# Two transformer blocks in one Trainium2 kernel: the silus of the first attention computed from the hyperbolic tangent, and its splits, gatings and table load at other steps

## The chip, the cores and the metric

The kernel runs on one core of a Trainium2 chip. The metric is the device time of one execution in microseconds (us), taken as the median of several runs. Five engines work side by side, each through its own queue in order: TensorE (PE in the profile, with its weight loads as PEld), VectorE (DVE), ScalarE (ACT), GpSimd (POOL) and SyncE (SP), which here only issues DMAs. They wait for each other through semaphores that count upwards.

## The reference, cut to what matters

A first block (a norm, one input projection, eight heads of a top-k attention "a" and eight heads of a dilated attention "b", a gating and an output projection) is followed by a second block and a final norm. What the change touches is the gating of the first block. `za` and `zb` are two slices of the input projection, and in the reference the attention output is multiplied by their silu before the output projection:

```python
def first_block(...):
    ...
    gated = concat(out_a, out_b) * silu(concat(za, zb))     # the gating, in short
    x = x + gated @ w_out
```

silu(z) is z * sigmoid(z), which equals z * 0.5 * (1 + tanh(z / 2)). Everything is float32; the kernel gets float32 accuracy on TensorE by writing each operand as a high part (fp32r) and a low part (the difference), and by three products: high with high, high with low, low with high.

## The kernel before, in words

Every engine's program is written out by hand in one function, `build`. The first attention is a loop over 64 steps (`steps1`), one step for one head and one tile of 128 queries: 8 groups of 8 steps, the first four groups for branch b and the last four for branch a. In a group the key width grows from 128 to 512 columns (two steps of each). All engines walk the steps in pairs (t = 0, 2, 4 ...):

- PE, step pair t: the scores of t and t+1 (`pair1`), which need that VectorE has taken the scores before them (`l_done`); then "fill" work, which is the projection of one of the eight tiles `zb 0..3`, `za 0..3` (`FILL1`), cut into single k chunks of three matmuls; then the transposes of the scaled probabilities of steps t-4 and t-3 (`turn1`, L1096); every fourth step the products with the values (`value1`, L1111). The transposes go alternately to two PSUM banks, so that the transpose of step u waits until VectorE has taken out the one of step u-2 (`t_free`, set by `turned_low`, L2222).
- ACT, step pair t: `turned_high(t-4)`, `turned_high(t-3)` (L1761, the high part of the transposed probabilities), `exps(t)`, `exps(t+1)` (L1578), sometimes `low_rows_of` (L1768), then what the tables put at t and t+1: `silu`, `high` (the high part of a weight unit, L1613), `wo_high` (the high part of a piece of `w_out`, L1747), and last `mixed_high` (L1730).
- DVE, step pair t: `score1(t)` (L2269), the reciprocal of the sums of t-2 and t-1 (L2277), `score1(t+1)`, `collect1` (L2230), `mix` (the gating, L2238), `gate_rows` (L2247 and L2248), `mixed_low` (L2254), `low` (the low part of a weight unit, L2090), `wo_low` (L2260), and then `turned_low(t-4)`, `turned_low(t-3)`.
- POOL, step u: the scaling of the probabilities by the reciprocal (L2752), which must be done before `turn1(u)`; in branch a also `combine(u+4)` (bias plus mask, L2739), which must be done before `score1(u+4)`; and at two steps `output_low` (L2746).
- SP: the loads. Weight unit number F0+n belongs to tile n of `FILL1`. Units F0+2 and later may be loaded only when PE has finished the tile two before it (`raw_free`), since they take its place in the ring.

The steps at which things happen are dictionaries from step to item. PE has filled the eight tiles at steps 8, 18, 26, 34, 41, 47, 53 and 59. `silu(tile)` runs in place on `zT` after `gate_rows`. `Silu` needs another activation table than `Exp`, and the silus were called in four pairs, at steps 20, 36, 49 and 63. The units' `high` parts were made at steps 10, 20, 28, 36, 43 and 49 (units F0+2 to F0+7), their `low` parts at step pairs 12, 22, 30, 38, 44 and 50, and that of F0+1 at 0. PE needs the units F0+1 to F0+7 at steps 10, 18, 27, 35, 42, 48 and 54.

Of the kernel before, what the change touches and what calls it, by code (L numbers as in the profile page):

```python
# [29 lines left out]
F32 = mybir.dt.float32  # L30
# [11 lines left out]
NH = 8  # L42
# [128 lines left out]
def build(nc, w, out):  # L171
# [29 lines left out]
    HIGH1 = {filled[tile] + 2: unit_of[tile] + 2 for tile in FILL1 if unit_of[tile] + 2 < U2}  # L201
    LOW1 = {1: F0 + 1, **{step // 2 * 2 + 2: u for step, u in HIGH1.items()}}
    GATE_AT = {tile: max(filled[tile], HALF + 8) if tile[0] == "za" else filled[tile] for tile in FILL1}

    SILU_AT = {min(filled[FILL1[2 * n + 1]] + 2, NS - 1) if n < 3 else NS - 1: n for n in range(4)}
    MIX_AT = {22: 0, 24: 1, 38: 2, 40: 3, 50: 4, 56: 5, 64: 6}
# [42 lines left out]
    with ExitStack() as ctx:  # L249
# [204 lines left out]

        def wo_raw(n, k, count=1):
            if n == 0:
                return v1["vb"][:, k:k + count, :] if k < 4 else qk1[:, 0, k - 4:k - 4 + count, K_LO, :]
            return late_raw[k // 2][:, k % 2:k % 2 + count, :] if k < 4 else qk1[:, 0, k - 4:k - 4 + count, OUTS, :]
# [96 lines left out]
        ki_lo_done = sem("ki_lo_done")  # L555
        z_done = sem("z_done")
# [938 lines left out]
        def _(act):  # L1495
# [213 lines left out]
            for g, done in zip(HEADED, (None, "kb", "qb", None, "ka", "qa")):  # L1709
                for k in range(3):  # L1710
                    if g != "va":
                        high(unit_of[(g, k)] + HI_UNITS)
                    if g == "kb":
                        for h in range(IDX_HEADS):
                            index_relu(k + 1, h)
                    if done is not None and k > 0:
                        head_high(done, 2 * k - 2)
                        head_high(done, 2 * k - 1)
                if g == "va":
                    high(F0)  # L1720
                for i in LAST_ORDER[g]:
                    take((g, i))
                high(F0 + 1 if g == "va" else unit_of[(g, 3)] + HI_UNITS)
                if g[0] != "v":
                    head_root(g)

# [22 lines left out]
            def silu(tile):  # L1749
                act.wait_ge(a_free, AT[tile] + 1)  # L1750
                z = zT[:, (0 if tile[0] == "za" else 4) + tile[1], :]
                run(z, z, ACT.Silu).then_inc(z_done, 1)
# [17 lines left out]
            for t in range(0, NS + 4, 2):  # L1770
# [10 lines left out]
                for u in (t, t + 1):  # L1781
                    if u in SILU_AT:
                        for n in range(2):
                            silu(FILL1[2 * SILU_AT[u] + n])
                    if u in HIGH1:
                        high(HIGH1[u])
                    if u in WO_HIGH:
                        wo_high(WO_HIGH[u])
# [255 lines left out]
        def _(dve):  # L2044
# [41 lines left out]
            def low(u):  # L2086

                dve.wait_ge(u_hi_done, u + 1)
                cols = unit_cols(u)
                v.tensor_tensor(u_lo[raw_place(u)][:, 0:cols], raw_unit(u),  # L2090
                                u_hi[hi_place(u)][:, 0:cols].bitcast(F32), ALU.subtract).then_inc(u_lo_done, 1)
# [142 lines left out]
            def mix(o, cols=slice(0, S)):  # L2234
# [3 lines left out]
                v.tensor_tensor(zT[:, k, cols], zT[:, k, cols], qk1[:, o // 4, o % 4, OUTS, cols], ALU.mult).then_inc(gated_done, 1)  # L2238

            def gate_rows(tile):  # L2240

                n = AT[tile]
                z = zT[:, (0 if tile[0] == "za" else 4) + tile[1], :]
# [28 lines left out]
            for t in range(0, NS + 4, 2):  # L2272
# [24 lines left out]
                for u in (t, t + 1):  # L2297
                    if u in LOW1:
                        low(LOW1[u])
# [387 lines left out]
        def _(pool):  # L2687
# [60 lines left out]

            for u in range(NS):
                if u % 2 == 0:  # L2750
                    pool.wait_ge(rden_done, u // 2 + 1)
                g.tensor_scalar(logits1[u % 8], logits1[u % 8], den[:, u:u + 1], unit_factor, ALU.mult, ALU.mult).then_inc(scaled, 1)  # L2752
                if u in (9, 11, 13, 15):
# [161 lines left out]
```

## Time and profile before

| what | value |
|---|---|
| median of 3 runs | 1031.36 us (1031.04 to 1031.43) |
| the profiled execution, its own time | 1029.16 us |
| its span in the trace | 1027.3 us |
| PE busy | 1005.7 us, 98% of the span |
| DVE, ACT, POOL busy | 680.4, 563.2, 422.8 us |
| mean granted TensorE clock | 0.999 |

How to read it: the span is the time between the first and the last instruction of the trace, and the profiled execution's own time is 1.9 us more. A busy engine counts only its work, not its waits. The first attention lies from about 170 to 300 us of the span. A row of a timeline gives start, duration, engine, source line, operation, tiles written and read, the shape, and in brackets how long the engine had been idle before it and who ended that. In the names, `x` is where the probabilities lie, `consts<-bank` is `low_rows_of`, and `arena<-arena` is a gating or a silu.

### The profile page before, as it was taken

The page shows a single profiled execution, that of the slowest core. Times are in us where ns is not written, and L with a number is a line of the kernel's source. Part 1 is how long each engine was busy: PE and PEld are TensorE (multiplying, and loading weights), DVE is VectorE, ACT ScalarE, POOL GpSimd, SP SyncE. Part 2 cuts the span into 40 slices and gives each one's busy share as a digit, 9 for nine tenths or more (in the row PEclk, how much of TensorE's full clock was granted, in tenths as well). Part 3 has the DMA queues.
Part 4 walks back from the last instruction along what each step waited for, and adds up shares of the span by engine and source line. Part 5 has one row for each costly group of instructions (what it writes and reads, how often), then busy time and mean ns, then how long its engine had stood idle before and what let it go on. Part 6 is the DMA issues. An engine that isn't in the chain of part 4 may idle for free. (4 is left out here: it accounts for less than half of the span.)

```text
span 1027.3 us, 14257 instructions
## 1 busy us (share of the span) xinstructions
PE 1005.7 (98%) x5150; PEld 826.2 (80%) x5150; DVE 680.4 (66%) x1207; ACT 563.2 (55%) x1032; POOL 422.8 (41%) x407
## 2 busy tenths in 40 slices
PE   9999999999989999999999999999999999999997
PEld 7788877777778898878887788888888888888885
DVE  5578997788974446824567879454322325999997
ACT  8455445778873355544567884234433446554564
POOL 0024011557840002900264430007779965874562
PEclk9999999999999999999999999999999999999999
DMA  9433321336140384233200362239999941443552
GB/s 336 104 98 109 88 67 36 83 83 191 56 175 1 103 267 143 60 82 83 63 2 1 121 229 62 82 111 323 347 352 349 356 168 62 153 143 135 205 185 82
DMA packets 100166, 146.25 MB, mean 142 GB/s; under 512 B 6480, under 2 KB 60496, under 8 KB 100096
## 3 DMA queue, kind: packets, MB, share of 16 engines
q1 hardware_dynamic: 86800, 130.75, 38.9%
q10 hardware_dynamic: 12768, 12.88, 4.0%
q0 software_dynamic: 528, 1.70, 0.9%
q8 instruction: 41, 0.67, 0.3%
q14 instruction: 29, 0.24, 0.1%
HBM read 123.69 MB, written 21.63 MB: 141 GB/s over the span
## 5 line engine op out<-in xcount | busy, mean ns | idle before, releaser
L2578 DVE TENSOR_TENSOR w_lo<-wring,w_hi 128x1024 fp32r<-128x1024 f32 x32 | 51.4, 1607 | 107.5 <-ACT w_hi L1944 107.5
L2090 DVE TENSOR_TENSOR u_lo<-wring,u_hi 128x1024 fp32r<-128x1024 f32 (+1 forms) x64 | 82.5, 1296 | 53.6 <-ACT u_hi L1613 52.9
L935 PE MATMUL bank<-u_hi,h_hi 128*128 128x512 f32 (+1 forms) x288 | 110.9, 385 | 0.1
L935 PE MATMUL bank<-u_hi,h_lo 128*128 128x512 f32 (+1 forms) x288 | 109.3, 379 | 0.0
L935 PE MATMUL bank<-u_lo,h_hi 128*128 128x512 f32 (+1 forms) x288 | 109.0, 378 | 0.0
L1613 ACT ACTIVATE u_hi<-wring 128x1024 fp32r<-128x1024 f32 (+1 forms) x64 | 66.2, 1034 | 69.4 <-PE bank L935 54.7
L935 PE MATMUL bank<-h_hi,w_hi 128*128 128x512 f32 (+2 forms) x272 | 103.2, 379 | 0.0
L935 PE MATMUL bank<-h_hi,w_lo 128*128 128x512 f32 (+2 forms) x272 | 103.1, 379 | 0.0
L935 PE MATMUL bank<-h_lo,w_hi 128*128 128x512 f32 (+2 forms) x272 | 103.1, 379 | 0.0
L935 PE MATMUL bank<-h_hi,u_hi 128*128 128x512 f32 x224 | 93.8, 419 | 0.4 <-ACT arena L1555 0.2
L1441 PE MATMUL bank<-s_hi,f_hi 128*128 128x512 f32 x224 | 87.4, 390 | 0.7 <-DVE f_lo L2612 0.7
L935 PE MATMUL bank<-h_lo,u_hi 128*128 128x512 f32 x224 | 87.7, 391 | 0.0
L935 PE MATMUL bank<-h_hi,u_lo 128*128 128x512 f32 x224 | 87.7, 391 | 0.0
L1442 PE MATMUL bank<-s_hi,f_lo 128*128 128x512 f32 x224 | 87.2, 389 | 0.0
L1443 PE MATMUL bank<-s_lo,f_hi 128*128 128x512 f32 x224 | 87.2, 389 | 0.0
L1944 ACT ACTIVATE w_hi<-wring 128x1024 fp32r<-128x1024 f32 x32 | 33.9, 1060 | 91.9 <-PE bank L935 91.9
L2804 POOL TENSOR_SCALAR arena<-arena,stats 128x128 f32<-128x128 f32 (+3 forms) x64 | 40.5, 642 | 95.0 <-DVE stats L2534 94.8
L2752 POOL TENSOR_SCALAR x<-x,stats 128x128 f32<-128x128 f32 (+3 forms) x64 | 49.4, 777 | 53.9 <-DVE stats L2277 53.9
L2604 DVE TENSOR_TENSOR s_lo<-wring,s_hi 128x2048 fp32r<-128x2048 f32 (+1 forms) x32 | 67.8, 2119 | 5.6 <-ACT s_hi L1974 5.6
L935 PEld LDWEIGHTS bank<-u_hi,h_hi 128*128 128x128 f32 x288 | 54.1, 188 | 11.5 <-issue 1.2
L935 PEld LDWEIGHTS bank<-u_lo,h_hi 128*128 128x128 f32 x288 | 54.1, 188 | 10.2
L1974 ACT ACTIVATE s_hi<-wring 128x2048 fp32r<-128x2048 f32 (+1 forms) x32 | 54.3, 1696 | 14.0 <-PE bank L1443 13.8
(382 smaller groups left out, 2600.2 us busy)
## 6 DMA issues: line engine op xcount, KB each, us to landing
wring<-in_w_in SPq DMA_DIRECT2D x60, 512.0 KB, 3.9
wring<-in_w_ff ACTq DMA_DIRECT2D x12, 1024.0 KB, 8.7
wring<-sums_kept SPq DMA_DIRECT2D x16, 768.0 KB, 4.2
wring<-in_w_ff SPq DMA_DIRECT2D x22, 512.0 KB, 6.2
wring<-in_w_ff SPq DMA_DIRECT2D x32, 256.0 KB, 3.3
sums_kept<-wring SPq DMA_DIRECT2D x22, 256.0 KB, 5.2
wring<-in_w_out SPq DMA_DIRECT2D x2, 2048.0 KB, 13.2
wring<-in_w_ff SPq DMA_DIRECT2D x4, 1024.0 KB, 6.9
```

Of the source, the lines that this page charges most:

```text
L935: last = mm(b, lhs, rhs, start=(start and n == 0), stop=(stop and n == 2))
L1441: mm(b, f[0][:, token], w[0][:, high], start=start, stop=False)
L1442: mm(b, f[1][:, token], w[0][:, high], start=False, stop=False)
L1443: return mm(b, f[0][:, token], w[1][:, lows], start=False, stop=stop)
L1613: run(u_hi[hi_place(u)][:, 0:unit_cols(u)], raw_unit(u), ACT.Copy).then_inc(u_hi_done, 1)
L1944: run(dst, src, ACT.Copy).then_inc(w_hi_done, 1)
L1974: run(s_hi[m % 4][:, 0:PAIR - at], pair_raw(m)[:, at:PAIR], ACT.Copy).then_inc(s_hi_done, 1)
L2090: v.tensor_tensor(u_lo[raw_place(u)][:, 0:cols], raw_unit(u), u_hi[hi_place(u)][:, 0:cols].bitcast(F32), ALU.subtract).then_inc(u_lo_done, 1)
L2578: v.tensor_tensor(cut(w_lo[ring3(m)]), src, cut(w_hi[ring3(m)]).bitcast(F32), ALU.subtract).then_inc(w_lo_done, 1)
L2604: v.tensor_tensor(s_lo[pair_place(m)][:, at:PAIR], pair_raw(m)[:, at:PAIR], s_hi[m % 4][:, 0:PAIR - at].bitcast(F32), ALU.subtract)
L2752: g.tensor_scalar(logits1[u % 8], logits1[u % 8], den[:, u:u + 1], unit_factor, ALU.mult, ALU.mult).then_inc(scaled, 1)
L2804: g.tensor_scalar(place, place, den2[:, u:u + 1], gates[:, i, at:at + 1], ALU.mult, ALU.mult).then_inc(scaled, 1)
```

## The change

- `silu` becomes `half_tanh`: ScalarE computes tanh(z/2) with `Tanh` and scale 0.5 into a place of its own (`tanh_place`, where a chunk of K's high part has been), waits for that on its own semaphore, adds 1 with `Identity` and a bias of one, and signals `tanh_done`. Before the first it waits until VectorE has taken every score of that chunk of heads (`l_done`), since PE reads that chunk until then. Tiles zb0 to zb3 and za0 to za3 come at steps 10, 20, 28, 36, 42, 48, 54 and 60, one at a time.
- GpSimd multiplies z with 1 + tanh (`gated`), behind the scaling of steps 12, 21, 29, 37, 45, 53, 61 and 62, and signals `z_done`.
- `mix` multiplies z with the attention output and with 0.5, by `scalar_tensor_tensor` in place of `tensor_tensor`. The gatings 0 to 3 move from steps 22, 24, 38, 40 to 18, 32, 34, 40, and with them `mixed_high` (two steps later) and `mixed_low` (four steps later). The others stay.
- The units' `high` parts come at steps 9, 19, 27, 35, 41 and 47, and so one step pair earlier than before.
- The units' `low` parts can be made in halves: F0+1 at 4 and 6 (before: 0), F0+2 at 10 (12), F0+3 at 20 and 22 (22), F0+4 at 28 and 30 (30), F0+5 at 38 (38), F0+6 at 42 and 46 (44), F0+7 at 50 (50).
- The table for `Exp` is asked for after the projection of `qa` instead of by the first `Exp`.

```diff
-    HIGH1 = {filled[tile] + 2: unit_of[tile] + 2 for tile in FILL1 if unit_of[tile] + 2 < U2}
-    LOW1 = {1: F0 + 1, **{step // 2 * 2 + 2: u for step, u in HIGH1.items()}}
+    HIGH1 = {filled[tile] // 2 * 2 + 1: unit_of[tile] + 2 for tile in FILL1 if unit_of[tile] + 2 < U2}
+    LOW1 = {4: (F0 + 1, 0), 6: (F0 + 1, 1), 10: (F0 + 2, None), 20: (F0 + 3, 0), 22: (F0 + 3, 1), 28: (F0 + 4, 0), 30: (F0 + 4, 1),
+            38: (F0 + 5, None), 42: (F0 + 6, 0), 46: (F0 + 6, 1), 50: (F0 + 7, None)}
...
-    SILU_AT = {min(filled[FILL1[2 * n + 1]] + 2, NS - 1) if n < 3 else NS - 1: n for n in range(4)}
-    MIX_AT = {22: 0, 24: 1, 38: 2, 40: 3, 50: 4, 56: 5, 64: 6}
+    TANH_AT = {10: 0, 20: 1, 28: 2, 36: 3, 42: 4, 48: 5, 54: 6, 60: 7}
+    GATED_AT = {12: 0, 21: 1, 29: 2, 37: 3, 45: 4, 53: 5, 61: 6, 62: 7}
+    MIX_AT = {18: 0, 32: 1, 34: 2, 40: 3, 50: 4, 56: 5, 64: 6}
...
+        def tanh_place(tile):
+            return qk1[:, 0 if tile[0] == "zb" else 1, tile[1], MIX_LO, :]
...
+                if g == "qa":
+                    nc.scalar.preload_act_table(ACT.Exp)
...
-            def silu(tile):
+            def half_tanh(tile):
                 act.wait_ge(a_free, AT[tile] + 1)
-                z = zT[:, (0 if tile[0] == "za" else 4) + tile[1], :]
-                run(z, z, ACT.Silu).then_inc(z_done, 1)
+                act.wait_ge(l_done, (0 if tile[0] == "zb" else HALF) + NH * (tile[1] + 1))
+                run(tanh_place(tile), gate_place(tile), ACT.Tanh, scale=0.5).then_inc(half_tanh_done, 1)
+                act.wait_ge(half_tanh_done, FILL1.index(tile) + 1)
+                run(tanh_place(tile), tanh_place(tile), ACT.Identity, bias=unit_factor).then_inc(tanh_done, 1)
...
-                    if u in SILU_AT:
-                        for n in range(2):
-                            silu(FILL1[2 * SILU_AT[u] + n])
+                    if u in TANH_AT:
+                        half_tanh(FILL1[TANH_AT[u]])
...
-            def low(u):
+            def low(u, part=None):
 
                 dve.wait_ge(u_hi_done, u + 1)
-                cols = unit_cols(u)
-                v.tensor_tensor(u_lo[raw_place(u)][:, 0:cols], raw_unit(u),
-                                u_hi[hi_place(u)][:, 0:cols].bitcast(F32), ALU.subtract).then_inc(u_lo_done, 1)
+                size = unit_cols(u) // (1 if part is None else 2)
+                cols = slice((part or 0) * size, (part or 0) * size + size)
+                done = v.tensor_tensor(u_lo[raw_place(u)][:, cols], raw_unit(u)[:, cols],
+                                       u_hi[hi_place(u)][:, cols].bitcast(F32), ALU.subtract)
+                if part != 0:
+                    done.then_inc(u_lo_done, 1)
...
-                v.tensor_tensor(zT[:, k, cols], zT[:, k, cols], qk1[:, o // 4, o % 4, OUTS, cols], ALU.mult).then_inc(gated_done, 1)
+                v.scalar_tensor_tensor(zT[:, k, cols], zT[:, k, cols], 0.5, qk1[:, o // 4, o % 4, OUTS, cols], ALU.mult, ALU.mult)\
+                    .then_inc(gated_done, 1)
...
+            def gated(tile):
+                pool.wait_ge(tanh_done, FILL1.index(tile) + 1)
+                z = gate_place(tile)
+                g.tensor_tensor(z, z, tanh_place(tile), ALU.mult).then_inc(z_done, 1)
...
+                if u in GATED_AT:
+                    gated(FILL1[GATED_AT[u]])
```

## Rows read from the trace of the kernel before

**Rows 1.** The page, busy time of the engines.
```profile
PE 1005.7 (98%) x5150; PEld 826.2 (80%) x5150; DVE 680.4 (66%) x1207; ACT 563.2 (55%) x1032; POOL 422.8 (41%) x407
```
**Rows 2.** Busy time by stretch: start, length, PE, PEld, DVE, ACT, POOL, clock, DMA.
```profile
245.00:262.00 17.00, 15.59 (x103) 12.45 (x102) 15.61 (x46) 14.36 (x33) 15.06 (x15) 1.00 0.55 151
...
sum 130.00, PE 120.00 PEld 95.09 DVE 106.30 ACT 103.25 POOL 83.30; mean PE 20.00 PEld 15.85 DVE 17.72 ACT 17.21 POOL 13.88
```
**Rows 3.** Waits of PE from 165 to 300: total, times, longest.
```profile
PE bank L1096 <- DVE pt_lo L2222: 4.5, 6, 1.3
PE bank L1086 <- DVE stats L2269: 3.9, 6, 1.4
```
**Rows 4.** Timeline of PE, instructions in front of which it stood idle.
```profile
175.24 0.79 PE L1086 MATMUL bank<-qk_half 64*128 64x384 f32 x6 [1.18 <-DVE stats L2269]
...
193.96 0.95 PE L1086 MATMUL bank<-qk_half 64*128 64x128 f32 x12 [0.71 <-DVE stats L2269]
...
209.83 0.85 PE L1096 MATMUL bank<-consts,x 128*128 128x128 f32 x6 [0.89 <-DVE pt_lo L2222]
...
214.18 1.09 PE L1096 MATMUL bank<-consts,x 128*128 128x128 f32 x8 [0.52 <-DVE pt_lo L2222]
...
254.81 0.96 PE L1086 MATMUL bank<-qk_half 64*128 64x128 f32 x12 [1.39 <-DVE stats L2269]
...
265.89 0.30 PE L1096 MATMUL bank<-consts,x 128*128 128x128 f32 x1 [1.05 <-DVE pt_lo L2222]
...
292.37 1.09 PE L1096 MATMUL bank<-consts,x 128*128 128x128 f32 x8 [1.35 <-DVE pt_lo L2222]
```
**Rows 5.** Groups by line and shape, 190 to 320: busy us, mean ns, idle before.
```profile
L2739 POOL TENSOR_TENSOR junk<-arena,x 128x512 f32<-128x512 f32 x8 | 10.3, 1285 | 0.0
...
L2090 DVE TENSOR_TENSOR u_lo<-wring,u_hi 128x1024 fp32r<-128x1024 f32 x9 | 12.5, 1391 | 3.5 <-ACT u_hi L1613 3.2
...
L1752 ACT ACT_TABLE_LOAD x4 | 5.1, 1283 | 0.1
...
L1752 ACT ACTIVATE arena<-arena 128x512 f32<-128x512 f32 x8 | 4.6, 624 | 0.0
```
**Rows 6.** DMA issue of unit F0+2, and its time from issue to landing.
```profile
L739 SPq DMA_DIRECT2D wring<-in_w_in x1: 368/368/368, 182.1 to 182.1; - x1
...
DMA to landing us min/median/max: 4.6/4.6/4.6
```
**Rows 7.** The same of unit F0+6.
```profile
L739 SPq DMA_DIRECT2D wring<-in_w_in x1: 424/424/424, 240.7 to 240.7; - x1
...
DMA to landing us min/median/max: 7.4/7.4/7.4
```
**Rows 8.** ACT at steps 9 to 10 and 40 to 43.
```profile
183.62 0.40 ACT L1578 ACTIVATE x<-x,stats 128x128 f32<-128x128 f32 x1
...
186.23 1.09 ACT L1761 ACTIVATE pt_hi<-bank 128x512 fp32r<-128x512 f32 x2 [2.13 <-PE bank L1096]
...
242.93 0.39 ACT L1578 ACTIVATE x<-x,stats 128x128 f32<-128x128 f32 x1
...
248.20 1.06 ACT L1613 ACTIVATE u_hi<-wring 128x1024 fp32r<-128x1024 f32 x1
```
**Rows 9.** PE, the transposes of steps 8 and 9, and of 40 and 41.
```profile
188.77 0.38 PE L1096 MATMUL bank<-consts,x 128*128 128x128 f32 x2
...
248.09 0.38 PE L1096 MATMUL bank<-consts,x 128*128 128x128 f32 x2
```
**Rows 10.** POOL: two scalings, the second behind a gap.
```profile
250.74 2.04 POOL L2752 TENSOR_SCALAR x<-x,stats 128x256 f32<-128x256 f32 x1
...
256.47 0.77 POOL L2752 TENSOR_SCALAR x<-x,stats 128x512 f32<-128x512 f32 x1 [1.16 <-DVE stats L2277]
```
**Rows 11.** DVE, score of step 63.
```profile
285.77 0.69 DVE L2269 CUSTOM_DVE_ANT_0 x<-bank,junk 128x512 f32<-128x512 f32 x1
```
**Rows 12.** ACT, the last exponential before the score of step 63.
```profile
283.81 0.61 ACT L1578 ACTIVATE x<-x,stats 128x384 f32<-128x384 f32 x1
```

More of the change, by code:

```diff
@@ L453, in build, with gate_place @@
         mix_place = lambda k: (0, k - 4) if k >= 4 else (1, k)
+        def gate_place(tile):
+            return zT[:, (0 if tile[0] == "za" else 4) + tile[1], :]
+        def tanh_place(tile):
+            return qk1[:, 0 if tile[0] == "zb" else 1, tile[1], MIX_LO, :]
         def wo_raw(n, k, count=1):
@@ L555, in build @@
         ki_lo_done = sem("ki_lo_done")
+        half_tanh_done = sem("half_tanh_done")
+        tanh_done = sem("tanh_done")
         z_done = sem("z_done")
@@ L2237, in mix @@
                 dve.wait_ge(z_done, FILL1.index(("zb" if k >= 4 else "za", k % 4)) + 1)
-                v.tensor_tensor(zT[:, k, cols], zT[:, k, cols], qk1[:, o // 4, o % 4, OUTS, cols], ALU.mult).then_inc(gated_done, 1)
+                v.scalar_tensor_tensor(zT[:, k, cols], zT[:, k, cols], 0.5, qk1[:, o // 4, o % 4, OUTS, cols], ALU.mult, ALU.mult)\
+                    .then_inc(gated_done, 1)
             def gate_rows(tile):
                 n = AT[tile]
-                z = zT[:, (0 if tile[0] == "za" else 4) + tile[1], :]
+                z = gate_place(tile)
                 if tile == ("za", 0):
@@ L2298, in _ @@
                     if u in LOW1:
-                        low(LOW1[u])
+                        low(*LOW1[u])
                     if WO_HIGH.get(u - 2, 5) < 5:
@@ L2747, in output_low @@
                     .then_inc(wo_lo_done, 1)
+            def gated(tile):
+                pool.wait_ge(tanh_done, FILL1.index(tile) + 1)
+                z = gate_place(tile)
+                g.tensor_tensor(z, z, tanh_place(tile), ALU.mult).then_inc(z_done, 1)
             for u in range(NS):
```

## The prediction

> **What bounds the kernel now.** I read the page first. PE is busy for 98% of the span [rows 1], so no change to ACT, DVE or POOL can be worth more than the idle time of PE in the stage it touches. The busy time by stretches gives that bound: in the 130 us of the first attention PE works 120 us, at full clock, so that 10 us are open; DVE and ACT work 106 and 103 us, and POOL 83 [rows 2]. From 245 to 262 all four are over 84% busy [rows 2]. There is hardly slack, and what is late on one engine soon reaches PE. The waits of PE tell by whom it is held: 4.5 us in six waits by `turned_low`, which must free the bank for the next transpose, and 3.9 us in six waits by `score1` [rows 3]. The timeline then says where. The reader is to see seven places with 1.18, 0.71, 0.89, 0.52, 1.39, 1.05 and 1.35 us [rows 4]; they make 7.1 of the 8.4 us. Only some belong to silus. The one at 175 stands behind the first `Exp`'s table load; 209.8 and 214.2 follow the silus of step 20, 265.9 those of step 49, 292.4 those of step 63. The one at 194 follows a unit's low part on DVE, and the one at 254.8 a late `combine` on POOL.
>
> **The change part by part.** All times below are on the clock of the old trace, and a gain or a loss is how much earlier or later PE gets through the same work.
>
> *Table load and the first low part.* A table load takes 1.28 us [rows 5]. The first `Exp` no longer waits for one, and DVE's low part of F0+1 (1.39 us [rows 5]) no longer stands in front of the scores of step 2. Asked for in the projection, the load lies where ACT waits for PE anyway; without that cover it would cost its 1.28 us. The wait of 1.18 us [rows 4] goes: -1.2 us. The two halves of 0.7 us at 4 and 6 lie in gaps of DVE.
>
> *Silu to tanh on ACT.* Four pairs cost 4.6 us of silu and 5.1 us of table loads [rows 5], and three more loads of 1.28 us back to `Exp` (3.8): 13.5 us. Sixteen activations of about 0.62 us [rows 5], and some 0.1 us for a wait on the own result, make 10.7 us. ACT gains 3 us in sum and loses its four knots of 2.6 to 5 us. At step 20 this frees PE: of 0.89 and 0.52 I take -1.4 us (bounds 0 and -1.9: nothing, if the low half and `mixed_low`, which stand before `turned_low` at 22, hold it as long; or also the short waits beside it).
>
> I weigh a rule here. The table load's rows show 1283 ns and the next activation starts at its end. The Trainium skill (ScalarE: Activation LUTs, What ACT_TABLE_LOAD costs) gives 1283 ns as well, but adds a drain and says 2.66 us for each switch. By the rows seven loads are 9.0 us of ACT, by the page they would be 18.6; I go by the rows, which show no drain.
>
> *The high parts one step pair earlier.* This is where I expect the loss, for `high` waits for a DMA that starts only when PE has finished a tile, and everything behind it on ACT's queue waits too. Unit F0+2 is issued at 182.1 and lands 4.6 us later, at 186.7 [rows 6]. Before, ACT came to it at step 10, at 188.8. Now it comes at step 9, after the exponentials that end at 184.0 [rows 8]: ACT stands for 2.7 us and then needs 1.05. `turned_high(6)` starts at 187.8 instead of 186.2 [rows 8]. DVE also stands, for its low part at pair 10 waits for the high part (187.8) and takes 1.39 us [rows 5]; two `turned_low` of about 0.65 us end at 189.9 and 190.5. PE wants the transposes of 8 and 9 at 188.8 [rows 9] and gets the second at 190.5: +1.7. The tanh of zb0 adds 1.3 us behind it on ACT, in time for the next transposes. The wait at 194 (0.71 [rows 4]) came from the low part at pair 12 and is partly used up: net +1.0 us (bounds +0.3 and +1.5).
>
> F0+3, F0+4 and F0+5 have the queue to themselves, as F0+2 has, and land about when ACT arrives at steps 19, 27 and 35, where it has had `low_rows_of` in front: nothing, for the `high` then takes the place of waits of ACT for PE (up to +0.5 each if not).
>
> Unit F0+6 is the heavy one. It is issued at 240.7 and, behind 2 MB of `w_out` in the same queue, lands 7.4 us later, at 248.1 [rows 7]. Before, ACT started it at 248.2, at step 43, having hardly waited [rows 8]. At step 41 ACT comes at 243.3 [rows 8], or at 242.0 with its earlier steps. It stands for 5 to 6 us. Behind it wait `turned_high(38)` and (39), the exponentials of 42 and 43, the tanh of za0 and `mixed_high(3)`; DVE stands too, in the first half of the low part at pair 42. So: high part until 249.2; `turned_high(38)` 249.8; DVE's half low part 249.9, `turned_low(38)` 250.6, (39) 251.2. PE wants the transposes of 40 and 41 at 248.1 [rows 9], and before that would have been 0.4 earlier: it gets the second at 251.2, over 3 us late. Value products, scores and fills up to the scores of 48 need 5 us as before, so PE is there at 256.2, and DVE's score of 47 is out at 256.6. At step 48 the old wait of 1.39 us [rows 4] for POOL shrinks, since PE is late itself: 256.6 against 254.8, net +1.8 us (bounds 0, if PE has other work to do, and +3.5).
>
> F0+7 at step 47 lands before ACT reaches it, but stands before `wo_high(1)` and `turned_high(44)`; DVE's `wo_low(1)` stands behind that, and at pair 50 DVE still has gating, low part (1.39 us [rows 5]) and `wo_low` in front of `turned_low(46)`, about 3 us. So the gain from the silus of step 49 (1.05 [rows 4] and a second wait of 0.30) doesn't come out whole: +0.8 us (bounds -1.35 and +1.5).
>
> *The last tanh.* The tanh of za3 stands at step 60, but waits for the score of step 63, since it writes over K. That score ends at 286.5 [rows 11]; ACT has ended its exponentials of 60 and 61 at 284.4 [rows 12]. It stands for 2 us, then needs 1.3, and `wo_high`, `turned_high(58)`, (59) and the exponentials of 62 and 63 come 2.3 us late. By step 64 it is level with the old order, as two silus and their load (2.5 us [rows 5]) are gone there. But the exponentials are late for POOL, which now also has products in front of the scalings of 62 and 63 (1.29 us each [rows 5]), and `low_rows_of` ends only at 291.0; behind it on DVE stand `collect1`, gating 6 and `turned_low(60)`, 2.2 us. That is out at 293.2, and the transposes of 62 and 63 start at 293.2 instead of 292.4 [rows 4]: +0.9 us (bounds -1.0 and +2.5).
>
> *The products on GpSimd.* Eight of 1.285 us [rows 5], 10.3 us. Most stand where POOL waits for the next reciprocal (as the 1.16 us before 256.5 [rows 10]). The trace shows what they can do besides: a scaling of 256 columns took 2.04 us while DVE subtracted between SBUF tiles, one of 512 columns 0.77 [rows 10]. Each product may hold DVE, or be held, for up to 1.3 us. I take +0.4 us in all (bounds 0 and +5, half of the eight on the path). The gating by `scalar_tensor_tensor` has the same two SBUF inputs and columns as before; the trace has no such row with both in SBUF, and I take nothing (bounds: 0.1 us less or more for each of eight).
>
> The Trainium skill (SBUF — State Buffer, the physical ports) says that a VectorE instruction with two SBUF inputs and a GpSimd one that reads SBUF exclude each other for a whole instruction; by that rule, the trace agrees, with 2.04 for a scaling that the wider one did in 0.77. It speaks against the eight products: all on the path would be 10 us.
>
> *Sum.* -1.2 +1.0 -1.4 +1.8 +0.8 +0.9 +0.4 = +2.3 us. The profiled execution took 1029.16 us, which gives 1031.5; the median of the runs lies 2.2 above it, so 1033.7.
>
> **The rivals.** (1) *PE never feels the landings.* It ends on the other side. PE has the scores and the fills of a pair in hand, and the transposes wait for ACT with some slack. For it: ACT saves 3 us and its knots, and at 186 it had been idle for 2.1 us [rows 8]. Against it: banks are only two, and ACT's wait at step 41 is over 4.8 us. It decides if `turned_low(38)` ends by 248, which needs the landing 3 us earlier. Then: -1.2 +1.0 -1.4 -1.35 (265.9) -1.35 (292.4) = -4.3: 1027.1. (2) *The port.* Half of the products on the path, and scalings held by low parts: +5 more than the knots give, 1038. Speaks for it: 245 to 262 is nearly full on both [rows 2]. Against: their places are mostly gaps. (3) *Tanh doesn't share Exp's table.* The trace shows no tanh. Then there are 16 loads instead of 7 and a knot at each tile; even one us for each on PE gives +8, and 16 us of ACT at the most: 1042. (4) *Even.* Gains and losses cancel within a microsecond: 1031.4.
>
> The Trainium skill (ScalarE: Activation LUTs, Table sets: the hidden batching unit) puts tanh in the set of exp, so rival 3 is unlikely by it; no run here shows it yet.
>
> **How the numbers follow.** The forecast gets 0.50 with its own range 1031 to 1037, rival 1 0.25, rival 2 0.13, rival 3 0.04, rival 4 0.08. 0.2% is 2.1 us, about what a measurement of this kernel can tell. The forecast lies just outside of it: 0.28 slower, 0.20 within, 0.02 faster. Faster 0.27; same 0.20 + 0.08 = 0.28; slower 0.28 + 0.13 + 0.04 = 0.45. The range is 1026.8 to 1038.5: rival 1 with a little, and rival 2.
>
> **What would show it.** One table load before 170 and none between 175 and 300; no wait at 175; ACT idle for 2 to 3 us and for 5 to 6 us in front of `u_hi` L1613 (shifted lines) for units F0+2 and F0+6, released by the DMA; PE waiting about 3 us at the transposes of 40 and 41; ACT idle for about 2 us before the last tanh. It would be wrong if the unit lands early, if PE has work in between, or if the products stretch DVE's low parts and gatings by far more than 0.1 us each.

## The result, and the profile after

The changed kernel takes 1037.83 us (median of four runs, 1035.96 to 1040.39), the one before 1031.20 (1031.03 to 1031.43) beside it: a ratio of 1.0058, 95% interval 1.0042 to 1.0074. It is slower. Forecast were 1033.7, a range of 1026.8 to 1038.5, and slower as the likeliest of the three outcomes. The direction holds, the size is 4.1 us short: the time lies above the forecast's own range (1031 to 1037) and close to the 1038 of rival 2. The profiled execution took 1035.96 us, its span is 1034.1.

The busy time of the engines on the page after, beside [rows 1]:

```profile
PE 1008.9 (98%) x5150; PEld 828.8 (80%) x5150; DVE 681.0 (66%) x1211; ACT 558.8 (54%) x1033; POOL 436.9 (42%) x415
```

ACT has 4 us less to do and POOL 14 more, and that alone tells nothing. The busy time by stretch, beside [rows 2], does:

```profile
245.00:262.00 17.00, 12.59 (x84) 9.77 (x83) 12.01 (x31) 12.44 (x27) 11.63 (x14) 1.00 0.46 132
...
283.00:300.00 17.00, 13.36 (x77) 10.63 (x76) 12.14 (x30) 12.06 (x31) 15.29 (x16) 0.92 0.00 1
sum 130.00, PE 117.11 PEld 92.50 DVE 106.14 ACT 95.67 POOL 92.73; mean PE 19.52 PEld 15.42 DVE 17.69 ACT 15.95 POOL 15.45
```

From 245 to 262 PE works 12.6 of 17 us; before it worked 15.6 [rows 2]. All engines are less busy there, which is what a stretch looks like in which everything stands for one transfer. The last column but two of 283 to 300 is new: the granted clock of TensorE is 0.92, not 1.00.

PE's waits from 165 to 300, beside [rows 3]:

```profile
PE bank L1106 <- DVE pt_lo L2238: 9.6, 9, 2.5
PE bank L945 <- DVE u_lo L2104: 1.4, 1, 1.4
PE bank L945 <- POOL qk_half L2763: 1.0, 1, 1.0
PE bank L1096 <- DVE stats L2286: 0.6, 3, 0.2
```

The waits for scores fell from 3.9 us to 0.6; those for `turned_low` (L2238 now) rose from 4.5 to 9.6, and a wait for a unit's low part in `three` (L945, a fill) is new. (The transposes of `turn1` are L1106 now, the scores of `pair1` L1096, `high` L1623, `low` L2104.)

PE's timeline, where it stood idle, beside [rows 4]:

```profile
189.62 0.30 PE L1106 MATMUL bank<-consts,x 128*128 128x128 f32 x1 [0.90 <-DVE pt_lo L2238]
...
239.96 0.41 PE L1106 MATMUL bank<-consts,x 128*128 128x128 f32 x2 [1.08 <-DVE pt_lo L2238]
...
250.15 0.30 PE L1106 MATMUL bank<-consts,x 128*128 128x128 f32 x1 [2.48 <-DVE pt_lo L2238]
...
258.51 0.50 PE L945 MATMUL bank<-h_hi,u_hi 128*128 128x512 f32 x1 [1.39 <-DVE u_lo L2104]
```

The wait of 1.18 us at 175 is gone, and so are those at 209.8 and 214.2. The ones at 189.6 and 250.2 are the two that were forecast, behind F0+2 and F0+6: ACT stood for the load of the unit, and what PE needed stood behind it. Those at 240.0 and 258.5 were not.

To count gains and losses I take PE's matmuls by their number, 5150 in both traces, and subtract the start of each before from its start after. At some numbers (first line: the time in the old trace), in us:

```
old time       173.7  175.2  188.9  194.0  217.9  239.9  244.7  248.2  250.8  254.8  255.7  265.9  292.4  300.6  end
after           1.07  -0.18   1.35   0.79  -1.10   0.05  -0.43   2.55   2.67   1.36   2.82   3.57   4.87   5.67  6.81
```

I call these numbers offsets; only how an offset changes from one place to the next tells of a loss or a gain. 1.07 of it is there before the first changed instruction acts, and 1.14 comes after the first attention; between them lie 4.6 us.

ACT's timeline at the two landings and before the last tanh (a number in brackets is the idle time in front, and what ended it), beside [rows 8, 12]:

```profile
186.56 1.06 ACT L1623 ACTIVATE u_hi<-wring 128x1024 fp32r<-128x1024 f32 x1 [2.65 <-DMA wring<-in_w_in]
...
247.62 1.06 ACT L1623 ACTIVATE u_hi<-wring 128x1024 fp32r<-128x1024 f32 x1 [5.48 <-DMA wring<-in_w_in]
...
289.92 0.63 ACT L1764 ACTIVATE arena<-arena 128x512 f32<-128x512 f32 x1 [2.07 <-DVE stats L2286]
```

All engines in front of the two waits of PE that were not forecast (timeline, 236 to 240 and 256 to 259):

```profile
236.67 1.73 POOL L2769 TENSOR_TENSOR arena<-arena 128x512 f32<-128x512 f32 x1
...
237.17 2.31 DVE L2104 TENSOR_TENSOR u_lo<-wring,u_hi 128x1024 fp32r<-128x1024 f32 x1
...
239.40 0.74 DVE L2238 TENSOR_TENSOR pt_lo<-bank,pt_hi 128x256 fp32r<-128x256 f32 x2
...
256.64 1.27 POOL L2769 TENSOR_TENSOR arena<-arena 128x512 f32<-128x512 f32 x1
256.70 1.77 DVE L2104 TENSOR_TENSOR u_lo<-wring,u_hi 128x512 fp32r<-128x512 f32 x1
```

A low part of 1024 columns took 1.39 us in the mean of before [rows 5]; here it takes 2.31, and a half of 512 columns takes 1.77. Each time a product on POOL (L2769) has begun just before, and DVE is through about when a low part of normal length would be that had waited for the product's end (238.40 and 257.91). Behind it stand the `turned_low` or the fill for which PE waits: 1.15 and 1.46 us in the table.

The kernel before has such a pair already, where GpSimd makes a low part of the values (L2722), and so the price could have been read there. Its trace has (timeline, two places)

```profile
189.86 1.28 POOL L2722 TENSOR_TENSOR va_both<-arena,va_both 128x512 fp32r<-128x512 f32 x1
189.96 2.27 DVE L2090 TENSOR_TENSOR u_lo<-wring,u_hi 128x1024 fp32r<-128x1024 f32 x1
...
251.23 1.21 DVE L2090 TENSOR_TENSOR u_lo<-wring,u_hi 128x1024 fp32r<-128x1024 f32 x1
```

2.27 us where GpSimd's instruction had begun 0.1 us before, and 1.21 where it was GpSimd's scaling that took longer (2.04 us [rows 10]).

The Trainium skill (SBUF — State Buffer, SBUF: two separate sides) has the rule that was weighed in the prediction, and adds that whichever of the two engines starts first keeps the ports for its whole instruction. These rows agree.

Groups by line and shape, 190 to 320:

```profile
L2769 POOL TENSOR_TENSOR arena<-arena 128x512 f32<-128x512 f32 x8 | 10.7, 1335 | 0.0
...
L1766 ACT ACTIVATE arena<-arena,stats 128x512 f32<-128x512 f32 x8 | 5.8, 724 | 0.3
...
L1764 ACT ACTIVATE arena<-arena 128x512 f32<-128x512 f32 x8 | 5.0, 622 | 2.1 <-DVE stats L2286 2.1
...
L2254 DVE SCALAR_TENSOR_TENSOR arena<-arena 128x512 f32<-128x512 f32 x7 | 7.9, 1124 | 0.1
```

The products and the sixteen activations cost what was taken for them, nearly: 10.7 us on POOL against 10.3, and 10.8 on ACT against 10.7. What the products do to others is another matter: a gating on DVE takes 1124 ns in the mean, where the kernel before had 864.

Last, busy time by stretch around the place where the granted clock of TensorE fell:

```profile
293.50:297.17 3.67, 1.67 (x12) 1.18 (x10) 2.87 (x6) 2.33 (x6) 3.10 (x3) 1.00 0.00 0
297.17:300.58 3.41, 3.34 (x13) 3.09 (x14) 2.99 (x7) 1.96 (x5) 2.67 (x3) 0.50 0.04 11
300.58:304.00 3.42, 3.42 (x24) 3.12 (x24) 1.96 (x4) 2.62 (x6) 1.32 (x1) 1.00 0.93 367
```

PE had been busy for 1.67 of 3.67 us. Then the clock was 0.50 for 3.41 us, which is 1.2 GHz instead of 2.4: 13 matmuls where the next 3.42 us hold 24. The trace of the kernel before has no such stretch until 1025, when the work ends.

The four runs of the changed kernel, each with the mean granted clock of the run, get longer as it falls:

```
us       1035.96  1037.30  1038.36  1040.39
clock    0.997    0.995    0.993    0.992
```

The runs of before that stood beside the experiments (75 in three sets) have 0.999 in the median. They show the same: the 43 at 0.999 took 1030.5 us in the median, the 11 at 0.997 took 1033.0. So the kernel before has executions in which the clock falls too.

### The profile page after: what moved, and what is told of

Read it like the earlier page. It is cut to its first block and busy times, and to the rows that moved or that the text cites. A ratio compares the mean times of both kernels' runs of the same rounds, so it can differ in the third digit from the quotient of the medians.

```text
span 1034.1 us, 14278 instructions
## 1 busy us (share of the span) xinstructions
PE 1008.9 (98%) x5150; PEld 828.8 (80%) x5150; DVE 681.0 (66%) x1211; ACT 558.8 (54%) x1033; POOL 436.9 (42%) x415
## 5 line engine op out<-in xcount | busy, mean ns | idle before, releaser
L2104 DVE TENSOR_TENSOR u_lo<-wring,u_hi 128x1024 fp32r<-128x1024 f32 (+2 forms) x68 | 84.2, 1246 | 59.9 <-ACT u_hi L1623 59.1
L945 PE MATMUL bank<-u_hi,h_hi 128*128 128x512 f32 (+1 forms) x288 | 110.9, 385 | 0.1
L945 PE MATMUL bank<-u_hi,h_lo 128*128 128x512 f32 (+1 forms) x288 | 109.2, 379 | 0.0
L945 PE MATMUL bank<-u_lo,h_hi 128*128 128x512 f32 (+1 forms) x288 | 109.0, 378 | 0.0
L1623 ACT ACTIVATE u_hi<-wring 128x1024 fp32r<-128x1024 f32 (+1 forms) x64 | 66.2, 1035 | 79.0 <-PE bank L945 55.6
L945 PE MATMUL bank<-h_hi,w_hi 128*128 128x512 f32 (+2 forms) x272 | 103.2, 379 | 0.0
L945 PE MATMUL bank<-h_hi,w_lo 128*128 128x512 f32 (+2 forms) x272 | 103.1, 379 | 0.0
L945 PE MATMUL bank<-h_lo,w_hi 128*128 128x512 f32 (+2 forms) x272 | 103.1, 379 | 0.0
L945 PE MATMUL bank<-h_hi,u_hi 128*128 128x512 f32 x224 | 93.8, 419 | 1.8 <-DVE u_lo L2104 1.4
L945 PE MATMUL bank<-h_hi,u_lo 128*128 128x512 f32 x224 | 87.7, 391 | 0.0
L945 PE MATMUL bank<-h_lo,u_hi 128*128 128x512 f32 x224 | 87.6, 391 | 0.0
L945 PEld LDWEIGHTS bank<-u_hi,h_hi 128*128 128x128 f32 x288 | 54.1, 188 | 11.5 <-issue 1.2
L945 PEld LDWEIGHTS bank<-u_lo,h_hi 128*128 128x128 f32 x288 | 54.1, 188 | 10.2
L945 PEld LDWEIGHTS bank<-u_hi,h_lo 128*128 128x128 f32 x288 | 54.1, 188 | 9.4
```

Source lines behind the costliest of these rows:

```text
L945: last = mm(b, lhs, rhs, start=(start and n == 0), stop=(stop and n == 2))
L1623: run(u_hi[hi_place(u)][:, 0:unit_cols(u)], raw_unit(u), ACT.Copy).then_inc(u_hi_done, 1)
L2104: done = v.tensor_tensor(u_lo[raw_place(u)][:, cols], raw_unit(u)[:, cols], u_hi[hi_place(u)][:, cols].bitcast(F32), ALU.subtract)
```

## The experiments

Twelve kernels, five rounds each against the kernel before; four kernels at a time ran on one chip, each four on another. The ratio is the measure, for before's median is 1030.8 to 1031.1 us from one set to the next. "Offset" is how much later than in the old trace PE starts the same matmul, as in the table above.

**e1. The heavy landing alone.** The changed kernel with F0+6 at its old steps:

```
+    HIGH1[43] = HIGH1.pop(41)
-            ... 42: (F0 + 6, 0), 46: (F0 + 6, 1), 50: (F0 + 7, None)}
+            ... 44: (F0 + 6, None), 50: (F0 + 7, None)}
```

> The changed kernel with the high part of unit F0+6 back at step 43 and its low part whole at pair 44. Theory L (landing: high parts that come before their DMA hold ACT): ACT no longer stands in front of that high part, PE gets the transposes of 40 and 41 about 3.0 us earlier, 1.2 us of it comes back as the old wait at the scores of 48, net 1.8 us less than the changed kernel. Theory P (port: GpSimd's products and VectorE's subtractions shut each other out): the half low part at pair 46, which took 1.77 us behind the product, is gone and with it 1.4 us of waiting of the fill of step 48. Both: 3.2 us less, 1034.6. Only P true: 1036.4. Neither (the time is lost to the clock or elsewhere): unchanged, 1037.8.

Measured: 1032.91 us (1030.34 to 1034.09), ratio 1.0010 (0.9998 to 1.0023). Five of the 6 us are gone by this one edit, more than the 1.8 us that the sum had for it and the 3.2 expected here. The edit takes away two things, not one: the landing, and the half low part at pair 46 that met a product. In the two traces they make 3.1 us together. From 244.7 to 255.7 the offset rises by 3.25 in the changed kernel (1.79 by the landing, 1.46 by the low part) and by 0.18 here. The other 1.9 us are not in these two traces; the mean granted clock was 0.997 in the median of these twelve runs, against 0.994.

**e2. All units back.** The changed kernel with high and low parts of all units at the old steps, so that tanh, products and table load are what is left of the change:

```
-    HIGH1 = {filled[tile] // 2 * 2 + 1: ...}
+    HIGH1 = {filled[tile] + 2: ...}
-    LOW1 = {4: (F0 + 1, 0), 6: (F0 + 1, 1), 10: (F0 + 2, None), ...}
+    LOW1 = {1: (F0 + 1, None), **{step // 2 * 2 + 2: (u, None) for step, u in HIGH1.items()}}
```

> The changed kernel with the high and low parts of all units where they were before; tanh, products, gatings and table load as changed. Theory L: also the 1.0 us at F0+2 goes, so 1.8 + 1.0 = 2.8 us less, and 1.4 more by theory P at pair 46, minus about 0.6 for the low part of F0+1 in front of the scores of step 2: 1034.2 (1032.5 to 1036). If L alone were the whole loss, it would be faster than the kernel before, at or under 1030. If the products are the whole loss (P alone), it stays above 1036.

Measured: 1031.18 us (1029.67 to 1034.81), ratio 0.9999 (0.9987 to 1.0011). The 1.5 us at F0+2 are gone too: the offset at 188.9 is -0.26 after -0.27 at 175.2.

**e3. The unit steps alone.** The kernel before, silus and all, with the new `HIGH1`, `LOW1` and halves:

> The kernel before with only the new steps of the high and low parts (with the halves); silus, gatings and table load as before. Theory L: +1.0 at F0+2, +1.5 to 2.5 at F0+6, some of it back where silus no longer share a step with a high part: 1033.5 (1032.3 to 1035). Theory P alone: there are no products, so the halves are neutral or help, 1031.2 or less.

Measured: 1039.57 us (1038.23 to 1042.48), ratio 1.0078 (1.0060 to 1.0095). Slower by 8 us, about 6 more than expected. In its profiled execution the offset goes from 1.14 at 244.7 to 5.11 at 248.2 and 7.29 at 250.8, and the clock is at half for 6.8 us from 251.5 on and twice more for 3.4 us. The steps of the units alone account for the whole loss and more; the rest of the change won some of it back.

**e4. The table load alone.** The kernel before with the one line `nc.scalar.preload_act_table(ACT.Exp)` behind tile `qa`:

> The kernel before with only the table for Exp asked for after qa. The low part of F0+1 still stands in front of the scores of step 2, so of the 1.18 us in front of the scores of step 4 about 0.6 goes: 1030.6. If the table load alone was what PE waited for: 1030.1. If the wait was the low part's: 1031.2.

Measured: 1030.09 us (1028.95 to 1032.44), ratio 0.9987 (0.9977 to 0.9998). The offset falls by 0.7 at 175.2 and stays: a gain of 0.7 to 1.3 us.

**e5. The products' price, first try.** The changed kernel with the product cut to 8 columns, so that 504 of 512 columns of the gating product are left out:

```
-                g.tensor_tensor(z, z, tanh_place(tile), ALU.mult)...
+                g.tensor_tensor(z[:, 0:8], z[:, 0:8], tanh_place(tile)[:, 0:8], ALU.mult)...
```

> The changed kernel with the GpSimd product of each gate tile cut from 512 to 8 columns, so 504 of 512 columns of the gating product are left out. Theory (products on GpSimd and two-input DVE work on SBUF hold each other up): the low part of F0+5 after step 37 takes about 1.4 us instead of 2.31 and the half low part of F0+6 about 0.7 instead of 1.77, the transposes of step 36 come 1.15 us and the fill of step 48 about 1.4 us earlier, and the time is 1034.0 to 1035.5 us against 1037.8. Rival (those two places are late for another reason, so the products are hidden): 1037 or more.

Measured: 1037.67 us (1036.50 to 1038.73), ratio 1.0066 (1.0053 to 1.0078): nothing gained. By the number alone the theory of the ports would be dead. The trace says otherwise. Groups by line and shape, then the timeline of the landing and the stretches around it:

```profile
L2104 DVE TENSOR_TENSOR u_lo<-wring,u_hi 128x1024 fp32r<-128x1024 f32 x5 | 6.2, 1240 | 2.4 <-ACT u_hi L1623 2.2
L2104 DVE TENSOR_TENSOR u_lo<-wring,u_hi 128x512 fp32r<-128x512 f32 x6 | 4.2, 704 | 6.2 <-ACT u_hi L1623 6.2
```
```profile
248.14 1.06 ACT L1623 ACTIVATE u_hi<-wring 128x1024 fp32r<-128x1024 f32 x1 [6.92 <-DMA wring<-in_w_in]
...
250.67 0.45 PE L1106 MATMUL bank<-consts,x 128*128 128x128 f32 x1 [3.95 <-DVE pt_lo L2238]
```
```profile
246.45:250.12 3.67, 0.26 (x2) 0.00 (x0) 0.89 (x2) 1.98 (x4) 0.12 (x1) 1.00 0.63 229
250.12:256.95 6.83, 6.13 (x25) 4.93 (x26) 3.94 (x13) 5.01 (x15) 4.09 (x4) 0.50 0.00 0
```

The low parts are short again (1240 and 704 ns in the mean, by the same view 1457 and 885 in the changed kernel). So are the gatings: 825 ns, against 1124. Both losses of PE to a low part are gone: the offset rises by 0.08 us from 217.9 to 239.9 and by 0.19 from 254.8 to 255.7, where it rose by 1.15 and 1.46. That `scalar_tensor_tensor` as such costs nothing is shown with it, as 825 ns is no more than the 864 of `tensor_tensor` before.

What was won came back at the landing. The unit is issued at 240.6 and lands at 248.1; in the changed kernel it was 240.8 and 247.6. PE is 0.95 us earlier at 244.7 (0.54 of that was there from the start), and finds a gate that opens half a microsecond later. It waits 3.95 us instead of 2.48, and after that works for 6.8 us at half the clock. The offset goes from -1.38 at 244.7 to 3.07 at 248.2 and 5.25 at 250.8: 1.5 us more by the stall, 2.2 by the clock. By the runs' mean clock (0.9945 in the median, 0.994 in the changed kernel) the two kernels don't differ, so how much of it belongs to the clock in the median run is not shown.

**e6. The last tanh.** The changed kernel with it two steps later (`TANH_AT` 62: 7 and `GATED_AT` 63: 7):

> The changed kernel with the last tanh at step 62 in place of 60 and its product after step 63. Theory (ACT stands 2 us before the tanh of step 60 for the score of step 63, and PE gets the transposes of 62 and 63 late): the 1.3 us lost between 286 and 294 go, and with them perhaps the half clock behind them: 1035.3 to 1036.6 us against 1037.8. Rival (the loss there comes from the products or the low parts): unchanged, 1037.8.

Measured: 1035.63 us (1032.48 to 1036.37), ratio 1.0040 (1.0024 to 1.0055), 1.9 us less than the change by the ratio, with intervals that overlap. From 288.3 to 292.4 the offset falls by 0.9 where it rose by 1.5. Between 293.2 and 293.5 1.8 us are lost again, since POOL now has the product in front of the low part of `w_out` that PE needs next (timeline of this kernel):

```profile
301.57 0.47 PE L945 MATMUL bank<-za_half,qk_half 128*128 128x512 f32 x1 [1.54 <-POOL qk_half L2763]
```

**e7. Two products later.** The changed kernel with `GATED_AT` 39: 3 and 47: 4 in place of 37 and 45:

> The changed kernel with two of the eight products two steps later (zb3 after step 39, za0 after step 47), with the same work in all. If only where a product meets a low part of DVE matters, the losses of 1.15 us at the transposes of step 36 and 1.46 us at the fill of step 48 go: 1035.2 to 1036.4 us. If the port is so full in this stretch that the product meets other two-input work wherever it stands (gatings, collects), the loss moves with it: 1037.0 to 1038.5 us.

Measured: 1036.10 us (1034.22 to 1040.62), ratio 1.0057 (1.0037 to 1.0077). The median alone lies in the first expectation's range; by the ratio nothing changed, and six runs that lie 6 us apart settle no more. The trace shows why little was to be won, and neither expectation had the reason. The low part takes 1.21 us now, but the gating that needs the product waits for it, in front of everything on DVE. And the product of step 21, which was not moved, met the half low part of step pair 22 in this execution that it had missed in the changed kernel's (timeline, two places):

```profile
208.41 1.71 POOL L2769 TENSOR_TENSOR arena<-arena 128x512 f32<-128x512 f32 x1
...
208.90 1.76 DVE L2104 TENSOR_TENSOR u_lo<-wring,u_hi 128x512 fp32r<-128x512 f32 x1
...
211.14 0.30 PE L1106 MATMUL bank<-consts,x 128*128 128x128 f32 x1 [1.59 <-DVE pt_lo L2238]
...
244.61 1.30 POOL L2769 TENSOR_TENSOR arena<-arena 128x512 f32<-128x512 f32 x1
...
246.01 1.13 DVE L2254 SCALAR_TENSOR_TENSOR arena<-arena 128x512 f32<-128x512 f32 x1 [2.73 <-POOL arena L2769]
```

**e8. The best version.** The changed kernel with the units from F0+2 on at the old steps, F0+1 in halves at 4 and 6, and the last tanh and its product at 62 and 63:

> The changed kernel with the high parts and the low parts of the units from F0+2 on back at the steps of before, the low part of F0+1 in halves at 4 and 6, and the last tanh at step 62 with its product after 63. If stalls for landings and the last tanh are what made the change slow, this keeps the gains (1.2 us from the early table load, 1.4 us from the silus of step 20) and drops the losses: 1028.5 to 1030.0 us, ratio to before 0.998 to 0.999. Rival (the products on GpSimd and the clock take back what the silus gave): 1031, the same as before.

Measured: 1027.89 us (1027.03 to 1030.83), ratio 0.9972 (0.9962 to 0.9983). It beats both kernels, by 0.3% and 0.9%. The other four start from it.

**e9. The products' price, second try.** The same cut to 8 columns, where no landing stands behind:

> The kernel of the run before with the units back (1027.9 us) with the GpSimd product cut from 512 to 8 columns; 504 of 512 columns of the gating product are left out. In the changed kernel this cut gave nothing (1037.7), and there the time that it freed in front of unit F0+6 came back as a longer wait for its landing. Here no such wait stands behind. If the products cost PE about 2 us and only the wait hid that: 1025.5 to 1026.5 us. If the products are hidden anyway: 1027.5 to 1028.5.

Measured: 1026.02 us (1025.61 to 1028.83), ratio 0.9953 (0.9939 to 0.9966), 1.9 us less than with whole products by the ratio; the two intervals just touch. The traces say where. The offset rises by 0.67 from 217.9 to 239.9 in the best version and by 0.12 here. At 293.2 to 293.5, where the last product stands in front of the low part of `w_out` on POOL, it rises by 1.8 and here by nothing. Not all of the price is thus the ports'. From 265.9 to 270 the best version loses 1.5 us to the half clock; here the clock is at full until 1023. At the end the offset is -2.95 against 1.64, but the profiled execution of the best version was the slowest of its twelve.

**e10. F0+2 early.** The best version with `HIGH1[9] = HIGH1.pop(10)`, its low part at 10:

> The same kernel (1027.9 us) with the high part of F0+2 at step 9 and its low part at 10, as in the change, all else as it was. By the offset read in the changed kernel (1.5 lost at the transposes of 8 and 9, 0.55 won back): 1028.9 to 1029.2 us. If a later stage takes it up: 1027.9.

Measured: 1028.90 us (1027.46 to 1030.59), ratio 0.9978 (0.9968 to 0.9987). The intervals overlap, so the time alone doesn't settle it; the offset does: from 175.2 to 194.0 it rises by 0.82, against 0.17 in the best version. F0+2 alone costs 0.65 us, less than the 1.0 of the sum.

**e11. F0+6 early.** The best version with `HIGH1[41] = HIGH1.pop(43)` and its low part in halves at 42 and 46:

> The same kernel (1027.9 us) with the high part of F0+6 at step 41 and its low part in halves at 42 and 46, as in the change. By the stall alone (1.8 us on PE): 1029.5 to 1030 us. If the longer idle of PE also brings stretches at the half clock, 1.0 to 1.7 us each: 1031 to 1034 us, with a lower mean granted clock than the 0.997 to 0.998 of that kernel.

Measured: 1033.37 us (1031.74 to 1037.27), ratio 1.0025 (1.0012 to 1.0038), 5.5 us more than the best version. Stretches around the landing:

```profile
245.79:249.46 3.67, 1.25 (x6) 0.68 (x4) 0.71 (x2) 1.80 (x3) 1.15 (x2) 1.00 0.65 236
249.46:256.29 6.83, 5.95 (x25) 4.74 (x25) 4.03 (x12) 5.19 (x15) 4.09 (x4) 0.50 0.00 1
```

The stall raises the offset by 3.65 from 244.7 to 248.2, the slow clock by 2.19 more by 250.8, and 1.36 come back by 254.8, where the old wait for POOL was. Then 1.3 more are lost, for the half low part at pair 46 meets a product as in the changed kernel (timeline, all engines):

```profile
258.53 1.28 POOL L2771 TENSOR_TENSOR arena<-arena 128x512 f32<-128x512 f32 x1
258.57 1.79 DVE L2106 TENSOR_TENSOR u_lo<-wring,u_hi 128x512 fp32r<-128x512 f32 x1
...
260.41 0.50 PE L947 MATMUL bank<-h_hi,u_hi 128*128 128x512 f32 x1 [1.24 <-DVE u_lo L2106]
```

Together that is 5.8 us from 244.7 to 255.7, where the best version's offset rises by 0.2. Its twelve runs again go by the clock: the four at 0.992 to 0.994 took 1035.2 to 1037.3, the six at 0.996 and 0.997 1031.7 to 1033.8.

**e12. Product behind the low part of `w_out`.** The best version with the last product on POOL after `output_low(6)`:

> The same kernel (1027.9 us) with the last product on GpSimd behind the low part of w_out piece 6 instead of in front of it. PE waited 1.5 us for that piece at 293. If that wait is the product's: 1026.4 to 1027.0 us. If another wait (the branch's low part, 1.3 us) ends next to it: 1027.5 to 1028.0.

Measured: 1032.06 us (1029.48 to 1032.95), ratio 1.0003 (0.9993 to 1.0013): 3 us slower than the best version by the ratio, where 1 was to be won. The wait moved (timeline) and got longer:

```profile
291.40 1.28 POOL L2768 TENSOR_TENSOR arena<-arena 128x512 f32<-128x512 f32 x1
...
292.78 1.40 DVE L2253 SCALAR_TENSOR_TENSOR arena<-arena 128x256 f32<-128x256 f32 x1 [1.53 <-POOL arena L2768]
...
294.10 1.28 DVE L2237 TENSOR_TENSOR pt_lo<-bank,pt_hi 128x512 fp32r<-128x512 f32 x2
...
294.84 0.38 PE L1120 MATMUL bank<-pt_hi,va_both 128*128 128x256 f32 x1 [2.32 <-DVE pt_lo L2237]
```
```profile
291.84:295.51 3.67, 1.35 (x8) 0.87 (x8) 2.73 (x4) 1.90 (x5) 2.27 (x3) 1.00 0.83 290
295.51:298.92 3.41, 3.41 (x16) 3.22 (x15) 2.49 (x3) 0.97 (x3) 1.60 (x1) 0.50 1.01 402
```

On DVE the last gating waits for the product, and the last two `turned_low` stand behind it. PE waited 1.54 us for the low part of `w_out`; now it waits 0.32 there and 2.32 here, and the slow clock follows. From 292.4 to 300.6 the offset rises by 3.5 us, in the best version by 1.2: that is most of the 3 us. At the end of the profiled execution this version is nevertheless at an offset of 0.36, against 1.64 of the best version's; that one was the best version's slowest run, this one its second fastest. Its median clock is 0.995, against 0.9975.

## Why the prediction was right, and where its size was off

The range held, and that owes something to luck. The forecast's own range ended at 1037; the stated one reached 1038.5 only because it took in rival 2, the port, with 1038. The time looks like rival 2 and is not: the port cost PE 2.6 us and not 5, and the rest of the miss is the half clock, which no rival had, and time outside the first attention, which differs between executions. Of the 6.8 us between the two profiled executions 2.2 lie outside the part that the sum describes.

By its own steps, in the profiled execution (the differences of the first table):

- Table load and the first low part: -1.2 forecast, -1.25 measured; alone -0.7 to -1.3.
- The knots of step 20: -1.4 forecast, -1.9 measured, at the far bound.
- F0+2: +1.0 forecast, +0.97 measured (1.53 lost, 0.56 won back), 0.65 alone in e10. ACT stood for 2.65 us, forecast 2.7.
- F0+6: +1.8 forecast, +1.79 measured from 244.7 to 254.8. ACT stood for 5.48 us, PE for 2.48. The landing came at 247.6, half a microsecond before the forecast one.
- Steps 47 to 50: +0.8 forecast, +0.75 measured.
- The last tanh: +0.9 forecast, +1.3 measured from 265.9 to 292.4; ACT stood for 2.07 us, forecast 2.
- Products on GpSimd: +0.4 forecast, +2.6 measured at two places (1.15 and 1.46). **This is the term of the sum that was mis-sized.** The port was seen and a bound of 5 us given to it, but 0.4 was taken because the products stand mostly where POOL waits. It is DVE's side that counts: a product in POOL's gap costs when a low part that PE needs starts within it. e9 against e8 gives 1.9 us for all eight, where no landing stands behind, half clock and POOL's own queue included. The prediction's last sign of being wrong came true here: from e5 to the changed kernel the low parts grew from 1240 to 1457 ns and from 704 to 885, the gatings from 825 to 1124, "by far more than 0.1 us each".
- Tanh and the table of `Exp`: after the load at 152 none comes until 315; before had eight for `Exp` and silu in between. Rival 3 is out. The Trainium skill (ScalarE: Activation LUTs, Table sets: the hidden batching unit) says so of the tables, and the trace agrees.
- Rival 1, that PE never feels the landings, is out by e1, e10 and e11; rival 4, even, by the time itself.

The terms make +4.6 us from 173.7 to 300.6 with two that the sum did not hold: -0.48 at 244.7, where the late PE lost less to a later wait, and **+0.8 by the half clock** behind 297.2. Of the rest to +6.8, 1.07 lies ahead of the first changed instruction and 1.14 behind the first attention. That first part differs from one execution to the next (0.2 to 2.3 us in the twelve kernels' traces), and so does the last, from -1.0 to 1.9, with 4.2 in e3; neither is explained.

The clock is the part that the prediction did not have at all, and the profiled execution, at 0.997, shows the least of it. The median run, at 0.994, took 1.9 us more. A stretch at half the clock costs what can be read in the offsets: 2.2 us by 250.8 in e11 and in e5, 1.5 from 265.9 to 270 in e8. Where a wait of PE comes behind it, it can cost nothing: in e2 the offset goes from -0.99 at 255.7 to 0.60 at 262 and is back at -0.62 at 265.9, where the old wait is gone. That F0+6 is so dear (5.5 us in e11, 5.0 in e1, against 1.8 forecast) has two reasons beside the landing itself: the half low part that meets a product, 1.3 and 1.46 us in the traces, which belongs to the same edit, and the clock, 2.2 us in e11's trace. For e1 the clock's share is argued from the runs' mean clocks, not shown.

What stays open is why it falls at one idle stretch of PE and not at another. The trace of before has a wait of 1.39 us at 254.8 [rows 4] and keeps the full clock, while e2, e10 and e12 fall to half within 2 us of that place after two waits of about 0.95 and 0.75 us. But e1 and e8 have the same two waits there (0.93 and 0.76, 0.96 and 0.76) and fall only at the next wait, at 267.5 and 266.3. So the sum of the waits alone doesn't decide it. Adding idle or taking it away without moving other work was not tried.

## What to carry to other kernels

Price a stall by what comes behind it. Where several losses stand in a row before one gate that hardly moves with them (a DMA that landed at 247.6 or 248.1), they need not add: taking the first away gave nothing (e5), and the same edit gave 1.9 us once the gate was gone (e9). So take the gate away first, and read an experiment that "changes nothing" in the trace before its theory is dropped.

Work given to GpSimd is priced by what DVE starts while it runs, not by POOL's gaps, and an edit can carry two losses at once: count them in the trace before you name one (e1, e11). And a consumer moved ahead of its producer only moves the wait, to an engine on which more may be queued behind it (e7, e12).

On this PE-bound kernel 3.65 us of stall were followed by 2.2 us lost to the clock (e11). Read the granted clock of all runs beside their times.

## What the runs showed of the hardware that was not expected

- TensorE's granted clock fell from 2.4 to 1.2 GHz for 3.4 us after a stretch in which PE had worked 1.67 of 3.67 us, and for 6.8 us after 0.26 (e5) and 1.25 (e11) of 3.67. In the trace of the kernel before it did not fall inside the work.
- Whether a product holds up a low part can change from one execution to the next where the code is the same: the half low part at step pair 22 took 0.68 us in the changed kernel's trace, where the product began 1.1 us after it, and 1.76 in e7's, where the product had begun 0.5 us before it. No edit of e7 lies ahead of that place.
- An activation of 512 columns with its bias in a tile (`Identity`) took 724 ns, one without (`Tanh`) 622. The Trainium skill (ScalarE: Activation LUTs, What ACT_TABLE_LOAD costs) gives 93 ns for such an operand; the rows show 102.
